# Four and two plain tiles with nine and ten block pairs, reordered lists at the start of both feed-forward stages, and a norm factor by logarithm and exponential

## What is computed

```python
h = h + 0.5 * (silu(u @ w_gate) * (u @ w_up)) @ w_down     # u = rmsnorm(h, ffn1_norm)
h = h + merged(rmsnorm(h, mix_norm)) @ w_out
h = h + 0.5 * (silu(u @ w_gate) * (u @ w_up)) @ w_down     # u = rmsnorm(h, ffn2_norm)
```

## Time and profile before

| | before |
|---|---|
| median of 3 runs | 1016.45 us |
| the profiled execution | 1016.93 us |
| its span, first to last instruction | 1015.1 us |
| granted TensorE clock | 1.000 |
| PE busy | 1010.2 us, 100% |
| DVE busy | 806.5 us, 79% |
| ACT busy | 527.6 us, 52% |
| POOL busy | 338.0 us, 33% |
| DMA | 128.02 MB, mean 126 GB/s |

### The profile page before, as it was taken

How to read it: one execution, slowest core, us unless ns; L and a number is a source line. 1 busy time by engine, 2 the same in 40 slices (tenths; PEclk the granted TensorE clock), 3 DMA queues, 4 the chain that set the end, 5 groups by cost and what they waited for, 6 DMA issues and landing times.

```text
span 1015.1 us, 16269 instructions
## 1 busy us (share of the span) xinstructions
PE 1010.2 (100%) x6308; PEld 906.1 (89%) x6308; DVE 806.5 (79%) x1145; ACT 527.6 (52%) x914; POOL 338.0 (33%) x204
## 2 busy tenths in 40 slices
PE   9999999999999999999999999999999999999998
PEld 7889999998989888778888888888999999988897
DVE  6978889879986678636788875788798889799873
ACT  7634555555543353547877733464445555564331
POOL 1302334431041443444544553430143344320411
PEclk9999999999999999999999999999999999999999
DMA  6657567713233352221222232326676677133333
GB/s 213 208 131 188 169 182 184 204 55 124 88 101 105 115 165 83 84 83 63 75 71 63 65 103 70 117 87 159 161 195 188 168 182 211 64 105 103 104 105 104
DMA packets 43961, 128.02 MB, mean 126 GB/s; under 512 B 4464, under 2 KB 5744, under 8 KB 43888
## 3 DMA queue, kind: packets, MB, share of 16 engines
q1 hardware_dynamic: 38704, 108.90, 33.2%
q0 software_dynamic: 4896, 17.83, 10.2%
q10 hardware_dynamic: 288, 0.29, 0.1%
HBM read 124.91 MB, written 2.10 MB: 125 GB/s over the span
## 4 chain that ended last, share of the span: by engine, by line
PE 97%; DMA 1%; DVE 1%; SPq 0%; ACT 0%; issue 0%; DVEq 0%
PE psum L671 17%; PE psum L673 17%; PE psum L672 17%; PE psum L783 11%; PE psum L782 11%; PE psum L781 11%; PE psum L941 3%; PE psum L940 3%; PE psum L939 3%; PE psum L1095 1%; DMA h<-x_dram 1%; PE psum L1108 1%; DVE sum_of_squares L1893 1%; PE psum L1125 1%; PE psum L1126 1%
## 5 line engine op out<-in xcount | busy, mean ns | idle before, releaser
L1198 ACT ACTIVATE w_high<-w_raw 128x1024 fp32r<-128x1024 f32 x110 | 115.9, 1054 | 123.1 <-DMA w_raw<-weights_dram 79.5
L1750 POOL TENSOR_TENSOR w_low<-w_raw,w_high 128x1024 fp32r<-128x1024 f32 x50 | 123.0, 2465 | 112.4 <-ACT w_high L1198 90.9
L1750 POOL TENSOR_TENSOR w_low_in_place<-w_raw,w_high 128x1024 fp32r<-128x1024 f32 x27 | 68.6, 2541 | 195.9 <-ACT w_high L1198 195.9
L671 PE MATMUL psum<-u_high,w_high 128*128 128x512 f32 x240 | 96.9, 404 | 0.0
L673 PE MATMUL psum<-u_high,w_low 128*128 128x512 f32 x240 | 93.7, 391 | 0.0
L672 PE MATMUL psum<-u_low,w_high 128*128 128x512 f32 x240 | 93.5, 389 | 0.0
L1271 ACT ACTIVATE gate_and_up<-psum 128x256 f32<-128x256 f32 x102 | 38.7, 380 | 99.5 <-PE psum L783 63.1
L671 PE MATMUL psum<-hidden_high,w_high 128*128 128x512 f32 x222 | 86.6, 390 | 0.0
L672 PE MATMUL psum<-hidden_low,w_high 128*128 128x512 f32 x222 | 86.5, 389 | 0.0
L673 PE MATMUL psum<-hidden_high,w_low_in_place 128*128 128x512 f32 x222 | 86.4, 389 | 0.0
L671 PE MATMUL psum<-ffn_u_high,w_high 128*128 128x512 f32 x158 | 61.7, 390 | 0.0
(11 more groups left out here) (341 smaller groups left out, 3422.1 us busy)
## 6 DMA issues: line engine op xcount, KB each, us to landing
w_raw<-weights_dram SPq DMA_DIRECT2D x110, 512.0 KB, 3.5
gate_a<-weights_dram SPq DMA_DIRECT2D x17, 512.0 KB, 6.3
gate_s<-weights_dram SPq DMA_DIRECT2D x17, 512.0 KB, 3.6
gate_s<-weights_dram POOLq DMA_DIRECT2D x17, 512.0 KB, 7.1
up_a<-weights_dram SPq DMA_DIRECT2D x17, 512.0 KB, 5.0
up_s<-weights_dram SPq DMA_DIRECT2D x17, 512.0 KB, 3.6
up_s<-weights_dram POOLq DMA_DIRECT2D x17, 512.0 KB, 8.6
gate_a<-weights_dram SPq DMA_DIRECT2D x17, 256.0 KB, 5.5
```

What stands on the lines that cost most here:

```text
L671: pe.matmul(o, wh, xh, start=start, stop=False)
L1198: act.activation(high[:, s, :], raw[:, s, :], ACT.Copy).then_inc(high_done, 1)
L1750: pool.tensor_tensor(wlow[:, s, :], raw[:, s, :], high[:, s, :], ALU.subtract).then_inc(low_done, 1)
```

## The change

`PLAIN` goes from (6, 4) to (4, 2), so there are nine pairs in stage 1 and ten in stage 2, after 8 and 4 plain units. SP issues gate's first blocks at the very start (stage 1), or as soon as the last unit before stage 2 was used. The lists of ACT and DVE around the plain tiles are reordered. In the first pair of each stage DVE makes the up sums of the next pair after the scaling instead of before it. The norm factor becomes exp(-0.5 ln v) on ACT with a square beside it, and two operations on DVE; this holds for all three norms.

```diff
-PLAIN = (6, 4)
+PLAIN = (4, 2)
@@ SP
-            for u in range(SLOTS, U_DN1):
-                load_used(u)
-                if u == SLOTS + 4:
-                    gate_prologue(0)
-                if u == SLOTS + 5:
-                    gate_prologue_rest(0)
+            gate_prologue(0)
+            load_used(SLOTS)
+            load_used(SLOTS + 1)
+            gate_prologue_rest(0)
+            load_used(SLOTS + 2)
+            load_used(SLOTS + 3)
...
-            for u in range(U_GU2 + SLOTS, U_DN2):
-                load_used(u)
-                if u == U_GU2 + SLOTS:
-                    gate_prologue(1)
-                if u == U_GU2 + SLOTS + 1:
-                    gate_prologue_rest(1)
+            sp.wait_ge(unit_used, U_GU2)
+            gate_prologue(1)
+            gate_prologue_rest(1)
@@ ACT, root
-                act.activation(sq[:, 1, :], sq[:, 0, :], ACT.Sqrt).then_inc(root_ready, 1)
+                act.activation(sq[:, 1, :], sq[:, 0, :], ACT.Ln).then_inc(log_ready, 1)
+                act.wait_ge(log_ready, n + 1)
+                act.activation(rinv[:, :], sq[:, 1, :], ACT.Exp, scale=-0.5).then_inc(root_ready, 1)
+                act.wait_ge(root_ready, n + 1)
+                act.activation(acc[:, :], rinv[:, :], ACT.Square).then_inc(root_squared, 1)
@@ ACT, start of stage 1
             next_unit(U_GU1)
+            next_unit(U_GU1 + 1)
             root(0)
@@ DVE, norm_root
-                then(dve.reciprocal(rinv[:, :], sq[:, 1, :]))
-                newton(rinv[:, :], sq[:, 0, :], acc[:, :])
-                then(dve.tensor_tensor(rinv[:, :], rinv[:, :], acc[:, :], ALU.mult))
+                then(dve.scalar_tensor_tensor(out=acc[:, :], in0=acc[:, :], scalar=-0.5, in1=sq[:, 0, :],
+                                              op0=ALU.mult, op1=ALU.mult))
+                then(dve.scalar_tensor_tensor(out=rinv[:, :], in0=acc[:, :], scalar=1.5, in1=rinv[:, :],
+                                              op0=ALU.add, op1=ALU.mult))
@@ DVE, plain of stage 1, the new list
+                    plain_scaled(n, base, 0, F)
+                    plain_scaled(n, base, 1, F)
+                    sum_moving(n, NT2)
+                    unit_low(base + 7)
+                    plain_hidden(0, F)
+                    plain_hidden(1, F)
+                    weight_sums(g, gate_w)
+                    low_a1(g, gate_w)
+                    sum_moving(n, T3)
+                    sum_moving(n, T4)
+                    sum_low(n, NT1)
+                    plain_scaled(n, base, 2, F)
+                    sum_low(n, NT2)
+                    low_s2(g, gate_w)
+                    dve.wait_ge(unit_used, base + 2 * PLAIN[n] - 1)
+                    weight_sums(g, up_w)
+                    low_a1(g, up_w)
+                    low_s31(g, gate_w)
+                    plain_scaled(n, base, 3, F)
+                    low_s2(g, up_w)
+                    low_s31(g, up_w)
+                    plain_hidden(2, F)
+                    plain_hidden(3, F)
...
@@ DVE, pair
-                    dve.wait_ge(product, done(n, i, 6))
-                    weight_sums(g + 1, up_w)
-                    low_a1(g + 1, up_w)
+                    if not adds_first:
+                        dve.wait_ge(product, done(n, i, 6))
+                        weight_sums(g + 1, up_w)
+                        low_a1(g + 1, up_w)
...
+                if adds_first:
+                    weight_sums(g + 1, up_w)
+                    low_a1(g + 1, up_w)
                 if more:
                     low_s2(g + 1, gate_w)
                     low_s31(g + 1, gate_w)
```

More of the change, by code:

```diff
@@ L298, in layer_kernel @@
         init_done = sem("init_done")
+        log_ready = sem("log_ready")
+        root_squared = sem("root_squared")
         pw_high = sem("pw_high")
@@ L802, in a11 @@
                         pe.wait_ge(pair_scaled, 3 * g - 3)
+                    elif PLAIN[n] > 3:
+                        pe.wait_ge(F["up_scaled" if k else "gate_scaled"], PLAIN[n] - 3)
                     else:
-                        pe.wait_ge(F["up_scaled" if k else "gate_scaled"], PLAIN[n] - 3)
+                        pe.wait_ge(var_ready, 2 * n + 1)
                     multiply(x + k, w["a_h"][:, one], w["a_l"][:, one], block_of(fu_h, B11), block_of(fu_l, B11), True)
@@ L810, in a12 @@
                         pe.wait_ge(part_summed, 6 * g - 5 + k)
-                    else:
+                    elif PLAIN[n] > 2:
                         pe.wait_ge(F["up_scaled" if k else "gate_scaled"], PLAIN[n] - 2)
@@ L1288, in plain @@
                     sum_high(n, T3)
-                    next_unit(base)
+                    high_a1(g, gate_w)
                     gate_silu_tile(0, F)
[L1291 to L1295, removed]
                     high_s2(g, gate_w)
                     high_s31(g, gate_w)
-                    next_unit(base + 3)
-                    gate_silu_tile(2, F)
+                    sum_high(n, T4)
                     high_late(g, gate_w)
                 else:
-                    next_unit(base + 1)
                     for c in range(HALF, DT):
@@ L1308, in plain @@
                     gate_silu_tile(0, F)
+                    high_a1(g, gate_w)
                     gate_silu_tile(1, F)
                     sum_high(n, NT2)
-                    next_unit(base + 4)
+                    high_s2(g, gate_w)
+                    high_s31(g, gate_w)
                     sum_high(n, T3)
                     sum_high(n, T4)
+                    high_a1(g, up_w)
+                    high_s2(g, up_w)
                     gate_silu_tile(2, F)
[L1315 to L1322, removed]
                     high_late(g, gate_w)
+                    high_s31(g, up_w)
+                    return
                 high_a1(g, up_w)
@@ new lines, in plain @@
+                    low_a1(g, up_w)
[3 more added lines that the diff above has]
+                    plain_hidden(1, F)
+                    sum_low(n, T3)
+                    late_lows(g, gate_w)
+                    sum_low(n, T4)
+                    late_lows(g, up_w)
+                    return
+                else:
+                    plain_scaled(n, base, 0, F)
+                    plain_scaled(n, base, 1, F)
+                    sum_moving(n, NT2)
+                    unit_low(base + 7)
@@ L2027, in plain @@
                     plain_hidden(0, F)
-                    unit_low(base + 5)
-                    plain_tile(1)
+                    plain_hidden(1, F)
                     weight_sums(g, gate_w)
                     low_a1(g, gate_w)
[L2032 to L2045, removed]
@@ L2046, in plain @@
                     sum_moving(n, T3)
                     sum_moving(n, T4)
-                    unit_low(base + 8)
+                    sum_low(n, NT1)
                     plain_scaled(n, base, 2, F)
-                    sum_low(n, NT1)
                     sum_low(n, NT2)
+                    low_s2(g, gate_w)
+                    dve.wait_ge(unit_used, base + 2 * PLAIN[n] - 1)
+                    weight_sums(g, up_w)
+                    low_a1(g, up_w)
+                    low_s31(g, gate_w)
@@ L2052, in plain @@
+                    plain_scaled(n, base, 3, F)
+                    low_s2(g, up_w)
+                    low_s31(g, up_w)
                     plain_hidden(2, F)
-                    unit_low(base + 9)
-                    plain_scaled(n, base, 3, F)
+                    plain_hidden(3, F)
                     sum_low(n, T3)
+                    late_lows(g, gate_w)
                     sum_low(n, T4)
-                    plain_hidden(3, F)
-                    unit_low(base + 10)
-                    weight_sums(g, gate_w)
@@ L2114, in pair @@
                 more = i + 1 < PAIRS[n]
+                adds_first = not i
                 def add_part(to, bank, pos, copied):
```

3 lines of the change are left out of this document (1 added, 2 removed).

## The result

| | median (lowest to highest) of | against the kernel before |
|---|---|---|
| before | 1016.56 us (1016.32 to 1017.04), 6 executions | |
| after | 1021.8 us (1019.97 to 1022.79), 6 executions | 1.0048 [1.0038, 1.0058] |

The profiled execution of after took 1022.06 us, its span 1020.2 (before's span: 1015.1). So the change is slower by 5.2 us, outside the range of the prediction, which had put "slower" last.

The account below looks back on a forecast made before the run. PE was taken as the bound, busy for 100% of the span. 1016.93 - 3.20 (tiles) + 1.9 (stage 1 stall) + 0.3 (second pairs) = 1015.93, median 0.48 lower: 1015.4 us; range 1013.2 to 1018.6.

Parts of the forecast that it names:

- The gain of the tiles: PE, both stages: a pair in place of two plain tiles saves 1.60 us each, 3.20 us in all.
- PE's due times: Stage 1's first pair, begun at 51.26: PE wants a11 of up at 54.14 and s2 of gate at 57.02.
- The chain from gate's sum: Stage 1: DVE's list ends with hidden tile 2 at 58.4, ACT's copy follows, PE stalls 1.9 us before s2 of gate.
- The term for the second pairs: Pairs behind the first, both stages: PE may wait for ACT's copy behind `first_tile`; 0.3 us together, ends 0 and 3.
- the term for gate's sum: Stage 1: POOL issues the adding DMA from 36.6, 5.45 us to DVE's use, so the sum is there at 42.1.
- Up's sum: Stage 1: load to use 9.3 us, there at 49.8 and up to 1.5 more; DVE arrives at 51.1, at worst 0.4 added.
- The adding DMA is slow: Rival, stage 1: landing after 8.8 puts gate's sum at 45.4, stall 5.3, time 1018.9; chance 0.19, alone or with others.
- Unit 5's high part: Stage 1, ACT: made first, 0.95 us, which puts the norm factor's table load to about 27.3.
- 1 MB of gate blocks: Stage 1 loads behind x and the first units, in idle queue time: no cost unless they delay unit 5.
- Two table loads: Rival: Ln and Exp share no table, 1.28 more ahead of unit 6; stall 3.2, time 1016.7; within the forecast's 0.47.
- Stage 2: First pair at 692.4: `rinv` at 681.8, up's load to use 9.3, low a1 at 694.1, due 695.3; no stall, by 1.2.
- It pays for the shorter lists: New norm factor, stage 1: worth nothing by itself on PE's path; ends near 32.6 on DVE, five us earlier.

Follow-up runs that it names:

- mix: adds_hidden with gate's low s2 in stage 1 moved behind up's low a1 and hidden tile 2 on DVE: 1014.09 us, ratio 0.9976 to the kernel before.
- early_order: Changed kernel, gate's adding DMAs ahead of unit 6's low part (stage 1), up's first ahead of gate's second (stage 2): 1016.42 us, 0.9998 to before.
- spin: Changed kernel with 34 useless matmuls ahead of a11 of up in stage 1's first pair: 1021.39 us, ratio 1.0045 to the kernel before.
- norm_old: Changed kernel with the old norm factor (square root, reciprocal, Newton step) put back: 1021.93 us, ratio 1.0049 to the kernel before.
- fixed_norm_old: fixed with the old norm factor (square root, reciprocal, Newton step): 1020.42 us, ratio 1.0035 to the kernel before.
- hidden_first: Changed kernel with stage 1's hidden tile 2 made right behind up's low a1 on DVE: 1020.24 us, ratio 1.003 to the kernel before.
- adds_hidden: Changed kernel with the edits of early_order and hidden_first together: 1014.46 us, ratio 0.9981 to the kernel before.
- fixed: adds_hidden with unit 7's low part on POOL (stage 1) and gate's low s31 behind up's low a1 (stage 2): 1015.4 us, 0.9993 to the kernel before.

## Why the prediction was wrong

**What was right.** The gain of the tiles, 3.20: mix has before's waits and is 3.0 shorter. The bound (PE alone, everything else by its lists) and PE's due times: a11 of up at 54.0, said 54.14. The chain from gate's sum through DVE's list and hidden tile 2 to ACT's copy. early_order shows it nearly bare: DVE begins gate's sums at 42.92 where 42.1 was said, 0.8 later, and PE loses 0.6 + 2.1 = 2.7 us where 1.9 was said, 0.8 more. The waits of after alone would never have shown this place. The term for the second pairs, 0.3 with ends 0 and 3, came out as no wait.

**The step that failed** is the term for gate's sum: "the sum is there at **42.1**". It was there at 46.24, 4.1 us later, because POOL issued the adding DMA at 39.69, not 36.6, and it took 6.55 us to its use, not 5.45. All of DVE's list stood behind it. The list itself was right: from gate's sum to the end of up's low a1 it was to take 11.7 us, and it took 12.1, of which 0.40 is the wait for up's sum. So low a1 came at 58.4, not 53.8, 4.4 us past its due time, and PE went on with s2 of gate at 63.81, not 58.9. The loss of stage 1 was 6.9, not 1.9: 4.1 for gate's sum, 0.4 for up's, and 0.5 in small pieces (0.1 each in DVE's list, in PE's due time and in the clock, 0.2 from the hidden tile to PE).

With it failed the second sum: "Up's sum: ... now 40.5 + 9.3 = 49.8, and up to 1.5 more ... so at worst 0.4 is added". The load was issued at 40.46, as said, and 0.40 is what DVE waited, but that agreement is luck: DVE came at 55.32 where 51.1 was said, and the sum at 55.72, 15.3 us behind the issue. I had taken load, add and use over as one number from a place where nothing else moved, though the same text had rows of 8.2 to 8.8 for an adding DMA with company. Both halves were in company: the load behind gate's two adding DMAs, the second add behind the load of a22. A DVE that came at 51.1 would have stopped here. early_order brings both forward, and the wait falls from 4.3 to 0.6.

**The rival that was nearly right.** "The adding DMA is slow" had gate's sum at 45.4 and a stall of 5.3. The sum came at 46.24, more by a late issue (3.1) than by a slow landing (1.1), and with the 0.8 between and up's 0.4 that rival gives 6.5 of the 6.9. What it didn't follow is where PE stops: by its own list up's low a1 ends 3.3 us behind 53.8, past 54.14, so PE stops at a11 of up first, and the copy's wait lies behind that.

**What made the issue late.**
- Unit 5's high part: it was to end in time for a table load at 27.3, which came at 29.31, 2.0 later. ACT idled 1.91 us for unit 5's load, issued at 23.69 (23.11 before) and landed in 4.5 us (3.4 before). "1 MB of gate blocks ... costs nothing unless it delays unit 5" names the condition and gives it no price. Whether those blocks slowed the load is not shown: in mix, with the same blocks, it landed in 3.5 us, and the table load came at 28.17.
- Two table loads, 1.28 more. I had it as a rival and took one, by no row. The Trainium skill, "ScalarE: Activation LUTs", section "Table sets: the hidden batching unit", says that ln then exp takes one load; here it is two, in each kernel with the new factor (31.26 above). The drain of 1.38 that the Trainium skill adds for every switch (the same page, section "What ACT_TABLE_LOAD costs") is not to be seen: 29.31 + 1.28 = 30.59, and the operation starts at 30.61. Leaving it out was right.

**Stage 2** was to have no stall, by 1.2 us, and had 1.1. Two terms were short there too. DVE had `rinv` 4.7 us behind the variance, not 3.5, with the second table load in between, so it came to up's sum with its slack used up. Then it waited for the sum, which it used 11.85 behind the load's issue at 687.11, not 9.3:

```profile
698.96 0.69 DVE L1978 TENSOR_TENSOR up_s<-up_s,up_a 128x512 f32<-128x512 f32 x1 [0.78 <-DMA up_s<-weights_dram]
```

**What was not in the sum at all:** that a stall lowers the clock. In after it cost little beyond the copy's wait, as spin shows, but norm_old and fixed_norm_old show the 0.50 behind waits of 1.8 to 2.7. norm_old alone has two such places, and its time is after's though its waits for up's low part are 1.1 us less.

**"It pays for the shorter lists"** is right for DVE and wrong for ACT in stage 1: the new factor put 2.6 us more of ACT's work ahead of unit 6, and so ahead of the adding DMAs. Both together gave the 0 of norm_old.

**Open:** why waits of near 2 us lower the clock in some executions and not in others (below); what the load and the adding DMA each pay for the other; whether another way to place the logarithm and the exponential would save a table load (not tried).

## What to carry to other kernels

Follow a transfer not by one duration from issue to use, but link by link, and ask of each what else is in flight then; a duration taken in a quiet stretch is the lower end, not the value. When PE waits for a late part, read the idle times of the engine that makes it: the transfer that it stood still for can be another one, far up its list. Where a list is pulled earlier, issue its transfers earlier as well: here a small operation ahead of two DMA issues on POOL, itself waiting for ACT, decided 5 us. And look for the chain behind the first wait: of two in series, the second alone brought 1.6 us (hidden_first), the first alone 5.4 (early_order), both together 7.3 (adds_hidden).

## What the runs showed of the hardware

- **Loads and adding DMAs hinder each other.** The same 512 KB load, issued at 40.4, landed 4.4 us later where gate's adding DMAs had been issued at 31.9 (early_order) and 8.0 us later where they were issued from 39.7 on (after). The Trainium skill, "DMA: Bandwidth & Descriptors", section "SWDGE vs HWDGE vs iDMA", has each DMA engine take turns between its queues; that fits, but no run here shows how they are shared.
- **Ln and Exp in sequence took two table loads of 1.28 us**, and the operation behind a load starts 0.01 to 0.02 after it (after, 29.31 to 32.55).
- **The clock after a wait.** In the traces it fell to 0.50, for 3 to 7 us, after waits of 4.3 (after) and 2.7 (fixed_norm_old), and after 1.8 (norm_old) and 2.1 (spin). It stayed at 1.00 after 2.1 (early_order), 1.9 (fixed) and 0.9 (stage 2 of after). So waits of near 2 us do both. early_order's window with its wait:

```profile
58.00:60.00 2.00, 0.10 (x1) 0.13 (x2) 1.32 (x2) 0.59 (x3) 0.00 (x0) 1.00 0.97 182
```

- **One kernel's executions differ in it.** The mean granted clock of each execution is on record. Of fixed's eleven, seven are at 1.000 and took 1014.35 to 1015.88 us, four are at 0.998 and took 1017.07 to 1017.57. Of early_order's eleven, only the slowest (1018.04) is at 0.998. All of mix's nine are at 1.000, and they lie 1.3 us apart where fixed's lie 3.2. So the clock falls in some executions of a kernel and not in others, and those are about 2 us slower. Only one execution of each kernel was traced, so what decides it is not shown.
